# A three-buffer rate projection with SyncE stores, and the first head pair prepared among the rate tiles

## The reference, cut to what matters

```python
r, k, v = lerp(0) @ w_r, lerp(2) @ w_k, heads(lerp(3) @ w_v)
g = lerp(5) @ w_g
xw, xa = lerp(1), lerp(4)
for d in range(2):
    w_log = -softplus(-(w0[d] + tanh(xw @ w1[d]) @ w2[d])) - 0.5
    dec = exp(-exp(w_log))
    a = sigmoid(a0[d] + (xa @ a1[d]) @ a2[d])
kk = heads(k * k_k); kk = kk * rsqrt(sum(kk * kk) + 1e-12)
# then a scan over the tokens, per head and direction, from r, dec, k, v, kk, a
```

## Time and profile before

| | us |
|---|---|
| median of 3 runs | 4376.29 |
| lowest and highest run | 4373.87, 4385.46 |
| the profiled execution's own time | 4385.46 |
| its span from first to last instruction | 4385.5 |
| PE busy | 3906.8 (89%) |
| DVE, ACT, POOL busy | 2038.8, 951.1, 716.3 |
| all 64 stores of the features are issued between | 2016.2 and 2420.9 |
| first rate tile evicted, at | 2359.33 |
| `ends(0)` starts, at | 2461.61 |

### The profile page before, as it was taken

The page is one execution under the profiler, slowest core; times in us unless marked ns, Lnnn a source line. Parts: engine busy times, 40 slices in busy tenths (PEclk is TensorE's granted clock), DMA queues, the critical chain, the costliest instruction groups (busy, mean ns, idle before and its releaser), DMA issues. The chain is left out here.

```text
span 4385.5 us, 73324 instructions
## 1 busy us (share of the span) xinstructions
PE 3906.8 (89%) x32380; PEld 2568.3 (59%) x32380; DVE 2038.8 (46%) x3237; ACT 951.1 (22%) x1721; POOL 716.3 (16%) x571
## 2 busy tenths in 40 slices
PE   5999999969999989787999588887888999999986
PEld 2458885434788855444555477777754555554432
DVE  2547723355584259924100254544413444540593
ACT  2411100000110020111002343443312444440101
POOL 0024441000445300000001432223000000100000
PEclk8999999989999999898997699999999999999997
DMA  1123323422432212111223211111021111111120
GB/s 59 41 100 137 103 88 133 173 96 96 143 136 87 75 40 67 39 38 74 94 87 117 84 44 43 38 34 33 8 86 51 56 53 51 44 60 48 57 86 19
DMA packets 113232, 320.00 MB, mean 73 GB/s; under 512 B 8032, under 2 KB 75616, under 8 KB 101152
## 3 DMA queue, kind: packets, MB, share of 16 engines
q1 hardware_dynamic: 104592, 280.87, 18.4%
q0 software_dynamic: 8336, 34.61, 2.3%
HBM read 278.75 MB, written 30.41 MB: 70 GB/s over the span
## 5 line engine op out<-in xcount | busy, mean ns | idle before, releaser
L745 PE MATMUL lin_ps<-hn,ring 128*128 128x512 f32 (+1 forms) x4448 | 1488.1, 492 | 98.3 <-DVE hn L2027 32.3
L745 PEld LDWEIGHTS lin_ps<-hn,ring 128*128 128x128 f32 x4448 | 847.0, 192 | 694.9 <-issue 612.1
L745 PE MATMUL lin_ps<-arena,ring 128*128 128x256 f32 (+3 forms) x3184 | 1017.4, 486 | 38.7 <-DVE arena L2383 24.8
L745 PEld LDWEIGHTS lin_ps<-arena,ring 128*128 128x128 f32 (+2 forms) x3184 | 614.7, 195 | 417.5 <-issue 327.9
L745 PE MATMUL lin_ps<-arena 64*64 64x64 f32 (+4 forms) x9344 | 596.8, 252 | 101.8 <-DVE arena L2299 33.9
L1523 ACT ACTIVATE arena<-lin_ps 128x512 f32<-128x512 f32 (+4 forms) x535 | 282.3, 548 | 1364.7 <-PE lin_ps L745 1364.3
L745 PEld LDWEIGHTS lin_ps<-arena 64*64 64x64 f32 (+1 forms) x9344 | 454.5, 143 | 188.4 <-issue 91.3
L2027 DVE SCALAR_TENSOR_TENSOR arena<-arena,vec 128x512 f32<-128x512 f32 (+2 forms) x563 | 436.5, 851 | 149.3 <-PE lin_ps L745 148.0
L2027 DVE SCALAR_TENSOR_TENSOR arena<-arena,cs 128x512 f32<-128x512 f32 x336 | 326.9, 1042 | 0.0
L745 PE MATMUL sum_ps<-arena 64*64 64x64 f32 x7136 | 296.7, 223 | 23.9 <-issue 14.1
L745 PEld LDWEIGHTS sum_ps<-arena 64*64 64x64 f32 x7136 | 257.2, 137 | 29.9 <-issue 16.6
(11 more groups left out here) (205 smaller groups left out, 3585.3 us busy)
## 6 DMA issues: line engine op xcount, KB each, us to landing
ring<-w_up SPq DMA_DIRECT2D x32, 1024.0 KB, 6.0
ring<-w_down SPq DMA_DIRECT2D x32, 1024.0 KB, 5.2
arena<-w_mod SPq DMA_DIRECT2D x24, 1024.0 KB, 8.0
arena<-w_mod SPq DMA_DIRECT2D x12, 2048.0 KB, 8.1
features<-arena POOLq DMA_DIRECT2D x64, 384.0 KB, 2.6
ring<-w_attn SPq DMA_DIRECT2D x16, 1536.0 KB, 6.5
ring<-w_conv_in SPq DMA_DIRECT2D x16, 1024.0 KB, 5.9
ring<-features SPq DMA_DIRECT2D x40, 384.0 KB, 3.3
```

Of the source, the lines that this page charges most:

```text
L745: return pe.matmul(out, lhsT, rhs, start=start, stop=stop)
```

## The change

The rate tiles get a third PSUM buffer, `sum_ps` (`lora_ps`), and tile n now waits for the eviction of tile n-3. Their 32 stores are issued by SyncE and counted in four semaphores of their own (`rated`). The weights of the way up and `twa` move to another place in SBUF (over `hpad`, which is free when the last of the six token mixes, "lerps", is done), so that the ring slot into which head pair 0 is loaded is free early. The masks and the parameters are loaded before the rate tiles. After store number 5, SyncE waits for the first four rate stores and all earlier ones and issues the seven loads of head pair 0; the other 26 stores come behind them in its list. On TensorE, ScalarE and GpSimd the preparation of head pair 0 stands after the rate tiles of `lora_up(3)` and around those of `lora_up(4)`. The diff, cut to its core:

```diff
+        rated = [sem(f"rated{b}") for b in range(4)]
...
-        twa = at(21536, 2, ALL)
+        w_up2, twa = at(0, 2048), at(2048, 2, ALL)
+        lora_ps = [lin_ps[:, 0, :], lin_ps[:, 1, :], sum_ps[:, :]]
...
+                if name == "lora":
+                    sp.wait_ge(lin_mm, prev[s.slot(0)])
+                    sp.dma_start(ring[:, s.slot(0), 0:2048], t["w_lora"][0, :, :]).then_inc(full[s.slot(0)], 16)
                     sp.dma_start(wmask, t["wkv_masks"]).then_inc(in_ready, 16)
                     sp.dma_start(par, t["wkv_par"].rearrange("j p c -> p j c")).then_inc(in_ready, 16)
-                    raws(0)
-                    sp.dma_start(wv, row_of(2, 0)).then_inc(value_in, 16)
+                    sp.wait_ge(lerp_ready, 48)
+                    sp.dma_start(w_up2, t["w_lora"][1, :, :]).then_inc(full[s.slot(1)], 16)
+                    for m in range(STORES):
+                        sp.wait_ge(lin_ev, s.tile(0, 2 + m) + 1)
+                        sp.dma_start(scratch[4 + m % 4, m // 4], staging[:, m % 4, :]).then_inc(rated[m % 4], 16)
+                        if m == 5:
+
+                            for b in range(4):
+                                sp.wait_ge(stored[b], 16 * KD)
+                                sp.wait_ge(rated[b], 16)
+                            raws(0)
+                            sp.dma_start(wv, row_of(2, 0)).then_inc(value_in, 16)
+                    prev[s.slot(0)], prev[s.slot(1)] = s.tile(0, s.free[0]), s.tile(0, s.free[1])
+                    continue
+                if name == "wkv":
+                    for b in range(4):
+                        sp.wait_ge(rated[b], 16 * KD)
...
+            def lora_up(j):
+
+                s = S["lora"]
+                if j == 0:
+                    pe.wait_ge(full[s.slot(1)], s.full(0, 1))
...
                 for q in range(4):
-                    n, rows = 2 + 4 * j + q, slice(64 * (q % 2), 64 * (q % 2) + 64)
-                    pe.wait_ge(lin_ev, s.tile(0, n) - 1)
+                    m_, rows = 4 * j + q, slice(64 * (q % 2), 64 * (q % 2) + 64)
+                    if m_ >= 3:
+                        pe.wait_ge(lin_ev, s.tile(0, m_ - 1) + 1)
                     for c0, cw in SEGS[ALL]:
-                        m = mm(lin_ps[:, s.buf(n), 256 + c0:256 + c0 + cw],
-                               ring[rows, s.slot(1), 1024 * (q // 2) + P * j:1024 * (q // 2) + P * j + P],
+                        m = mm(lora_ps[m_ % 3][:, 256 + c0:256 + c0 + cw],
+                               w_up2[rows, 1024 * (q // 2) + P * j:1024 * (q // 2) + P * j + P],
                                twa[rows, q // 2, c0:c0 + cw], True, True)
                     m.then_inc(lin_mm, 1)
...
-            pe.wait_ge(lin_ev, S["lora"].tile1)
...
+            for j in range(4):
+                lora_up(j)
             key_sums(0)
+            lora_up(4)
             for part in range(2):
                 key_spread(0, part)
             for part in range(2):
                 values(0, part)
+            for j in range(5, KD):
+                lora_up(j)
+            pe.wait_ge(lin_ev, S["lora"].tile1)
             bonus_sums(0)
             ready_ends(0)
             ends(0)
...
-                act.wait_ge(stored[b], 16 * turn)
+                if turn > KD:
+                    act.wait_ge(rated[b], 16 * (turn - KD))
+                else:
+                    act.wait_ge(stored[b], 16 * turn)
                 act.wait_ge(lin_mm, s.tile(0, tile) + 1)
-                f(staging[:, b, :], lt(s.buf(tile), ALL), func, **kw).then_inc(lin_ev, 1)
+                ps = lora_ps[(tile - 2) % 3][:, 256:1024] if name == "lora" else lt(s.buf(tile), ALL)
+                f(staging[:, b, :], ps, func, **kw).then_inc(lin_ev, 1)
...
+            act.wait_ge(lerp_ready, 48)
...
-            reset_f(0)
-            reset_e(0)
+            for j in range(4):
+                lora_rates(j)
+            act.wait_ge(wkv_zero, 1)
+            act.wait_ge(in_ready, 16 * (LOADS + 2))
+            act.wait_ge(par_ready, 1)
             key_squares(0)
-            key_roots(0)
             key_gains(0, 0)
             key_gains(0, 1)
+            key_roots(0)
             for d in range(2):
                 decays(0, d)
             decay_ends(0)
             read_gains(0)
+            lora_rates(4)
             for part in range(2):
                 values(0, part)
+            for j in range(5, KD):
+                lora_rates(j)
+            reset_f(0)
+            reset_e(0)
+            for b in range(4):
+                act.wait_ge(rated[b], 16 * KD)
             for half in range(2):
...
+            for b in range(4):
+                dve.wait_ge(rated[b], 16 * KD)
...
-            order += [(4 + q, j, S["lora"].tile(0, 2 + 4 * j + q)) for j in range(KD) for q in range(4)]
...
-            for b in range(4):
-                pool.wait_ge(stored[b], 16 * n_st // 4)
...
+            pool.wait_ge(lerp_ready, 48)
...
+                    pool.wait_ge(lin_mm, S["lora"].tile1)
```

More of the change, by code:

```diff
@@ L521, in build @@
         spare_ps = lin_ps[:, 1, 512:1024]
+        STORES = 4 * KD
         def gram_part(n):
@@ L628, in _, with row_of @@
                 s = S[name]
[L629 to L640 removed]
+                def row_of(a, j):
+                    return scratch[a:a + 1, ds(j, 1), :, :].rearrange("a o p t -> p (a o t)")
@@ new lines, in raws @@
+                def raws(j):
+                    pace = 15 * j - 20
+                    for n, (to, a) in enumerate([(k_, 1), (ws[0], 4), (ws[1], 5), (wa[0], 6), (wa[1], 7), (r_, 0)]):
+                        if j and n and pace + n > 0:
+                            sp.wait_ge(z_mm, pace + n)
+                        sp.dma_start(to, row_of(a, j)).then_inc(raw_in[n], 16)
+                if name == "lora":
+                    sp.wait_ge(lin_mm, prev[s.slot(0)])
+                    sp.dma_start(ring[:, s.slot(0), 0:2048], t["w_lora"][0, :, :]).then_inc(full[s.slot(0)], 16)
@@ L1736, in _, with lora_rates @@
                 f(twa[:, n, :], lt(s.buf(n), ALL), func).then_inc(lin_ev, 1)
-            for j in range(KD):
+            def lora_rates(j):
                 for q in range(4):
```

17 lines of the change are left out of this document (1 added, 16 removed).

## The result

The changed kernel takes 4333.84 us (median of 4 runs, 4331.83 to 4336.31) against 4378.98 us (4 runs, 4373.87 to 4385.46) for the kernel before: a ratio of 0.9895, 95% interval 0.988 to 0.9909.

What follows compares the result with a forecast made beforehand. TensorE bounds the kernel; the change concerns 102.3 us from first rate eviction to `ends(0)`. The new terms put `ends(0)` at 2430.8 instead of 2461.6, saving 30.8 us: 4376.3 - 30.8 = 4346, range 4328 to 4360.

Steps and rivals of the forecast that it cites:

- if the clock is 1.00 among the rate tiles: One of the prediction's signs of failure; it expected TensorE's granted clock to stay 0.50 until behind `ends(0)`.
- Third buffer: Rate tiles: the 3.98 us buffer loop, shared by three buffers, gives 1.33 us a tile, before 1.97; 1.52 without overlap.
- The stall: Near tile 10: store 6 lands behind seven loads, holding ScalarE's evictions up about 5 us, bounds 2 to 8.
- ScalarE's preparation: Head pair 0, behind the sixteenth tile: ScalarE's part takes 10.2 us, then a sigmoid table load of 1.28 us.
- Spreads, keys, values: On TensorE behind tile 19: the chain keeps its 9.5 us, a new wait in which no rate tile runs.
- Tiles 20 to 31: Behind the values: 3.0 us for tile 20, eleven steps of 1.33 (14.6 us) and one eviction of 0.9.
- GpSimd covered with 14.5 us to spare: Beside the last twelve rate tiles: GpSimd's features are ready at 2416.3, 14.5 us before `ends(0)` needs them.
- What costs nothing: Around `ends(0)`: the last stores' wait and mask loads are hidden; 11.3 us before the key square leave the path.
- The clock comes back: Rival, chance 0.22: full clock in the rate tiles, pace 0.95 to 0.98 us; 8 us plus 7 more, time 4331.
- Heavier traffic: Rival, chance 0.13: rate tiles at 1.52 us and a stall of 8 us; 7 us less gain, time 4353.
- The store's round trip: Rival, chance 0.05: slow store landing binds the staging ring; slower by over 0.3% from 9.6 us landing, 4401 at 11.
- The gain is given back: Rival, chance 0.07: the scan's first groups wait for something later, such as head pair 1's loads; within 13 us of 4376.

## Why the prediction was right, and which term was off

The time lies in the range, and the path and most of the terms are right. But the forecast's own sign of failing came up: "if the clock is 1.00 among the rate tiles". It was, for most of tiles 4 to 9 and 20 to 31. The range holds because it had been drawn to take in that rival. Of the 12 us below the forecast, 5.3 come from the stretch (the last twelve tiles and the bonus sums 6.3 us shorter, the sixteenth tile 1.1 late) and 5.5 from the piece behind it, and both go back to the clock.

- *Where the bound lay: right.* Only the stretch and its clock changed, and every kernel's gain follows its stretch. The gain exceeds the shortening by 2.7 to 9.0 us, 4.8 in the middle, in the nine comparisons with the new order, and by 0.7, 1.0, 1.4 and 4.5 in the four with the old one, where the piece behind `ends(0)` is shortened by 2.0 to 3.3 us only.
- *Third buffer, 1.33 us a tile (bound 1.52): mis-sized, by the step on the clock.* The prediction put it as "granted clock 0.50 until behind `ends(0)`". Tiles 3 to 9 went at 1.01 and tiles 20 to 31 at 0.93, at a granted clock of 0.99 to 1.00 but for 3.4 us at the start of the first group and 1.9 of the second. Only tiles 10 to 15, at 0.50, went at the 1.31 of the forecast. The loop of "3.03 + 0.90 + 0.05" was right for the clock that it was read at; the fault was to hold that clock for a property of the tiles, on the ground that busy time of 59.3 in 61.3 us had not lifted it. "For it: the third buffer fills TensorE more densely" was the better argument, and had 0.22.
- *The stall, 5 us (2 to 8): mis-sized.* It was 8.6 us (8.9 with the wait ahead of it). The bytes were counted at 404 GB/s with nothing beside them. At 1.01 us a tile the stores fill the DMA engines themselves (share 1.01 in the kernel with the third buffer and SyncE's stores), so there was no room left over for the loads, as there would have been at 1.33; that this makes the whole difference is argued, no run shows it apart. Together with the fast tiles before it the sixteenth tile was done 26.3 us behind the first, where I had 25.2: two faults that cancel to 1.1 us, which is luck.
- *ScalarE's preparation, 10.2 us: right* (2384.06 to 2394.23), with the third table load of 1.28 us. Tile 19 is evicted 41.7 us behind the first eviction, forecast 40.6.
- *Spreads, keys, values, 9.5 us: right* (2399.35 to 2408.80), the new wait included, with the clock at 0.50 as before.
- *Tiles 20 to 31, 18.5 us: 13.6.* The same step on the clock. *Bonus sums, 2.9: 1.5*, the same again.
- *GpSimd covered with 14.5 us to spare: right in kind.* It took 10.98 us, as forecast, and was done at 2415.93, 8.0 us before `ends(0)`; the slack shrank because the twelve tiles that cover it went faster.
- *What costs nothing: right.* `raws(1)` is issued 1.7 us behind `ends(0)` (0.5 forecast), where it was 3.5.
- *Sum: 30.8 us, measured 36.1 in the stretch and 5.5 behind it.* The second piece has no term in the prediction, which let the 0.50 of the clock run on past `ends(0)` as before.
- *The rivals.* "The clock comes back" (4331) is nearest, though it came back in two pieces only: its gains on the spreads, the values and tile 19 didn't come, those behind `ends(0)`, which it doesn't count, did. "Heavier traffic" was half true: the stall was beyond its 8 us, the pace was not 1.52. "The store's round trip": SyncE's stores landed in 2.8 us (median), far from 9.6. "The gain is given back": 20.9 us behind `ends(0)`, nothing was late.

On the queues, the Trainium skill (DMA: Bandwidth & Descriptors, section on queues, rings and completion order) says that DMA engines alternate between the rings of different queues. The trace agrees in kind: with the loads on GpSimd's queue the one wait of 8.6 us became six of at most 3.3. Here it is no remedy, since their sum went from 8.9 to 8.4 us only, where the prediction put stores and loads on two queues near 2.

## What to carry to other kernels

When a stretch runs at the lower of the two clocks, its durations are no constants of the work: work out the sum for both clocks, and take the lower one only where the arrangement of the matmuls stays as it is. When tiles use half of the rows and alternate over two PSUM buffers, try a third buffer, or one wait more that starts the pair together; here the one gave 1.97 to 1.13 us a tile by itself and the other 3.97 to 3.40 us a pair. And ask of each store followed by a load of the same data whether the data can stay: with the DMA engines full, the kernel without eight such transfers of 384 KB had a stretch 7.6 us shorter (with the other moves of that edit), where a new place for the loads gave 3.5 at most.

## What the runs showed of the hardware that I had not expected

- A TensorE that the trace shows busy 34.00 of 34.00 us can be held at 1.2 GHz, and one busy 15.66 of 34.00 us can be granted 2.4 GHz for all but its first 0.3 us. The tiles were the same (64 rows, 128 columns of weights, float32); two staggered buffers gave the first, a pair that starts together and then leaves TensorE idle for 1.8 us gave the second.
- With three buffers the clock fell for 3.4 us at the start of the rate tiles and then came back, in each of the kernels that had three. In the changed kernel it fell once more in the stall behind tile 9 and stayed at 0.50 for 37.6 us, although the tiles went on with three buffers.
- The Trainium skill (TensorE: Matmul & The Clock Gate, section on a second failure mode, the depth-cycling of the PSUM queue) tells of short idle times between groups of matmuls that make the clock go back and forth. The runs differ from that here: staggered, without an idle time in the records, it stays low throughout, and in step, with 1.8 us without a matmul in every 3.4, it stays high.
